# A streaming-encoder block on one core: seven head pairs' attention probabilities turned by VectorE in squares of 32, convolution taps moved around them, and a second residual buffer

## The reference

```python
h = rms_norm(x)                                   # one projection of h gives c_q, c_kv, k_rope, u, gates
q = rms_norm(c_q) @ w_uq;  k, v = split(rms_norm(c_kv) @ w_ukv)      # per head; rope on 64 columns
s = (q k^T) * scale                               # for each block of 128 queries
p = softmax(where(chunk(key) <= chunk(query), s, -inf))              # chunks of 64 tokens
y_a = p v
u = silu(layer_norm(causal_depthwise_conv(a * sigmoid(g), 31 taps)))
x = x + (sigmoid(gA) * y_a + sigmoid(gB) * (u @ w_pw2 + b)) @ w_o
x = x + cross_attention(rms_norm(x), rms_norm(mem))
x = x + swiglu(rms_norm(x))
```

## Time and profile before

| | |
|---|---|
| median of 3 runs | 1668.11 us |
| lowest, highest | 1668.08, 1668.18 us |
| the profiled execution | 1668.08 us |
| its span, first to last instruction | 1666.3 us |
| busy: TensorE, VectorE, ScalarE, GpSimd | 1651.1, 1128.5, 822.7, 104.7 us |

### The profile page before, as it was taken

One profiled execution on the slowest core, in us unless ns is written; L12 is line 12 of the kernel. 1 busy time (PEld: TensorE's weight loads), 2 busy tenths in 40 slices (PEclk: granted clock), 3 DMA queues, 4 the chain that ended last, 5 costly groups with the idle time before them and its releaser, 6 DMA issues.

```text
span 1666.3 us, 23809 instructions
## 1 busy us (share of the span) xinstructions
PE 1651.1 (99%) x7760; PEld 1378.8 (83%) x7760; DVE 1128.5 (68%) x1461; ACT 822.7 (49%) x1049; POOL 104.7 (6%) x154
## 2 busy tenths in 40 slices
PE   9999999999999999999999999999999999999997
PEld 8888888888888888878888888888888888888886
DVE  5578777778986467986558856666666666654453
ACT  7556555556545444556555644444444444344343
POOL 3100100010000000120001200000000000000000
PEclk9999999999999999999999999999999999999999
DMA  7865555556676665554435666666666666565563
GB/s 231 246 206 161 173 166 155 169 158 176 176 214 184 192 213 177 187 191 155 147 127 196 188 196 191 193 195 190 191 185 191 201 197 194 194 217 182 184 213 133
DMA packets 161106, 309.68 MB, mean 186 GB/s; under 512 B 10240, under 2 KB 16896, under 8 KB 160800
## 3 DMA queue, kind: packets, MB, share of 16 engines
q1 hardware_dynamic: 158864, 301.50, 59.0%
q0 software_dynamic: 1488, 6.42, 1.0%
q10 hardware_dynamic: 704, 1.11, 0.2%
HBM read 306.89 MB, written 2.10 MB: 185 GB/s over the span
## 4 chain that ended last, share of the span: by engine, by line
PE 92%; DVE 4%; issue 2%; ACT 1%; DMA 0%; DVEq 0%; POOL 0%; ACTq 0%; POOLq 0%; SPq 0%
PE acc L365 28%; PE acc L367 27%; PE acc L366 27%; DVE w_lo L1261 2%; PE tp L377 1%; DVE x_f L1600 1%; PE acc L582 1%; PE acc L580 1%; PE acc L581 1%; PE sc L492 1%; ACT w_hi L786 0%; PE ov L516 0%; PE sc L497 0%; DMA raw<-in_w_in_dram 0%; PE sc L506 0%
## 5 line engine op out<-in xcount | busy, mean ns | idle before, releaser
L1261 DVE TENSOR_TENSOR w_lo<-raw,w_hi 128x1024 fp32r<-128x1024 f32 (+3 forms) x591 | 718.7, 1221 | 428.9 <-ACT w_hi L786 419.5
L786 ACT ACTIVATE w_hi<-raw 128x1024 fp32r<-128x1024 f32 (+3 forms) x591 | 605.8, 1027 | 758.3 <-PE acc L367 722.3
L365 PE MATMUL acc<-w_hi,crossT 128*128 128x512 f32 x832 | 324.8, 390 | 0.8 <-DVEq L1618 0.7
L367 PE MATMUL acc<-w_hi,crossT 128*128 128x512 f32 x832 | 323.9, 389 | 0.0
L366 PE MATMUL acc<-w_lo,crossT 128*128 128x512 f32 x832 | 323.8, 389 | 0.0
L365 PE MATMUL acc<-w_hi,mixT 128*128 128x512 f32 x732 | 289.4, 395 | 1.6 <-ACTq L881 0.7
L367 PE MATMUL acc<-w_hi,mixT 128*128 128x512 f32 x732 | 285.5, 390 | 0.0
L366 PE MATMUL acc<-w_lo,mixT 128*128 128x512 f32 x732 | 285.1, 389 | 0.0
L365 PEld LDWEIGHTS acc<-w_hi,crossT 128*128 128x128 f32 x832 | 156.2, 188 | 33.9 <-issue 1.5
L367 PEld LDWEIGHTS acc<-w_hi,crossT 128*128 128x128 f32 x832 | 156.2, 188 | 32.6
L366 PEld LDWEIGHTS acc<-w_lo,crossT 128*128 128x128 f32 x832 | 156.2, 188 | 32.1
(11 more groups left out here) (267 smaller groups left out, 1552.8 us busy)
## 6 DMA issues: line engine op xcount, KB each, us to landing
raw<-in_w_in_dram SPq DMA_DIRECT2D x104, 512.0 KB, 4.3
raw<-in_w_gate_dram SPq DMA_DIRECT2D x88, 512.0 KB, 4.3
raw<-in_w_up_dram SPq DMA_DIRECT2D x88, 512.0 KB, 3.8
raw<-in_w_down_dram SPq DMA_DIRECT2D x80, 512.0 KB, 4.1
raw<-in_w_kv_mem_dram SPq DMA_DIRECT2D x64, 512.0 KB, 4.0
raw<-in_w_o_dram SPq DMA_DIRECT2D x32, 512.0 KB, 4.1
raw<-in_w_q_mem_dram SPq DMA_DIRECT2D x32, 512.0 KB, 3.7
raw<-in_w_o_mem_dram SPq DMA_DIRECT2D x32, 512.0 KB, 3.7
```

What stands on the lines that cost most here:

```text
L365: mm(o, lo, whi, start=first and k == 0, stop=False)
L367: ins = mm(o, hi, whi, start=False, stop=end)
L786: fn(w_hi[:, s, 0:width], raw[:, s, 0:width], ACT.Copy).then_inc(hi_done, 1)
L1261: V.tensor_tensor(w_lo[:, s, 0:width], raw[:, s, 0:width], w_hi[:, s, 0:width].bitcast(F32), ALU.subtract).then_inc(lo_done, 1)
```

## The change

- TensorE's six turns and ScalarE's copy for pairs 0 to 6 go. VectorE instead turns `probs` into `probsT` in 16 instructions of 32 partitions x 192 elements (six squares of 32 each): 5 behind its low part of tile 9, 5 behind tile 10's, 6 behind tile 11's. The last one raises `probs_out`.
- TensorE's value products move from behind tile 7 to behind tile 8, VectorE's gating from tile 7 to tile 9.
- The 20 taps per pass stay 20; in passes 1 to 6 they now stand 3, 3, 2, 2, 2, 0, 0, 0, 3, 0, 3, 2 behind tiles 0 to 11 (before 0, 2, 1, 1, 2, 2, 2, 2, 2, 2, 2, 2).
- The scores of the next pair wait for `scores_read` instead of `probs_out`.
- Pair 7 keeps the old way (`LAST_PE`, `LAST_ACT`, `LAST_DVE`). One of the memory operand's parts moves from pass 7 (behind tile 9) into the memory stage.
- `x_f` gets a second buffer, laid in `row_bc`, and the turn waits for the low part of two chunks before; the `x_update` loops are written out on ScalarE, VectorE and GpSimd.
- In `pointwise` VectorE adds the bias to the first half before the low part of a tile, the second half behind it.

```diff
-PAIR_PE = {1: (0, 1), 3: (2,), 6: (5,), 7: (7,)}
-PAIR_ACT = {1: (0, 1), 4: (3,), 6: (5,)}
-PAIR_DVE = {3: (2,), 4: (3,), 7: (7,)}
+PAIR_PE = {1: (0, 1), 3: (2,)}
+PAIR_ACT = {1: (0, 1), 4: (3,)}
+PAIR_DVE = {3: (2,), 4: (3,), 5: (4,), 6: (5,), 7: (6,), 9: (7,)}
...
                     tile_products(i * 12 + T_C, 8 + t, t, 2, cqT, 2 * t, 2, UQ, i * 3 + (C_C + 1))
+                    if t == 0 and not first:
+                        attention(7, i - 1, i + (Q_C - 1))
...
+                if t in (4, 5, 6):
+                    if t == 4:
+                        dve.wait_ge(exp_done, 4 * p + 4)
+                        if not (isinstance(p, int) and p == 0):
+                            dve.wait_ge(pv_done, p)
+                    for n in range((0, 5, 10)[t - 4], (5, 10, 16)[t - 4]):
+                        i, j = n // 4, n % 4
+                        src = probs[32 * i:32 * i + 32, :, :].rearrange("p h (j c) -> p (h j) c", c=P)
+                        to = probsT[32 * j:32 * j + 32, :, :].rearrange("p h (j c) -> p (h j) c", c=P)
+                        ins = V.transpose(to[:, :, 32 * i:32 * i + 32], src[:, :, 32 * j:32 * j + 32])
+                    if t == 6:
+                        ins.then_inc(probs_out, 1)
...
-            share = [0, 0, 2, 3, 4, 6, 8, 10, 12, 14, 16, 18, EARLY_TAPS]
+            share = [0, 3, 6, 8, 10, 12, 12, 12, 12, 15, 15, 18, EARLY_TAPS]
...
-                    if last and t in (9, 11):
-                        operand_lo(t // 2 - 2)
+                    if last and t == 11:
+                        operand_lo(2)
...
                 for t in range(4):
-                    split_lo(c * 4 + T_D, t + 4)
...
-                        for b in range(NB):
-                            bias_added(b, c, c + C_D, c * 4 + (T_D + 4), free)
+                        bias_added(0, c, c + C_D, c * 4 + (T_D + 4), free)
+                    split_lo(c * 4 + T_D, t + 4)
+                    if t == 2:
+                        bias_added(1, c, c + C_D, c * 4 + (T_D + 4), free)
...
                     dve.wait_ge(stage_full, fills)
-                    dve.wait_ge(x_lo_out, done)
+                    if done >= 2:
+                        dve.wait_ge(x_lo_out, done - 1)
...
-            with dve.Fori(1, 4) as c:
+            for c in range(1, 4):
```

More of the change, by code:

```diff
@@ L50 @@
 EARLY_TAPS = 20
-PAIR_PE = {1: (0, 1), 3: (2,), 6: (5,), 7: (7,)}
-PAIR_ACT = {1: (0, 1), 4: (3,), 6: (5,)}
-PAIR_DVE = {3: (2,), 4: (3,), 7: (7,)}
+PAIR_PE = {1: (0, 1), 3: (2,)}
+PAIR_ACT = {1: (0, 1), 4: (3,)}
+PAIR_DVE = {3: (2,), 4: (3,), 5: (4,), 6: (5,), 7: (6,), 9: (7,)}
+LAST_PE = {1: (0, 1), 3: (2,), 6: (5,), 7: (7,)}
+LAST_ACT = {1: (0, 1), 4: (3,), 6: (5,)}
+LAST_DVE = {3: (2,), 4: (3,), 7: (7,)}
 HEAD_PE = {0: (0,), 2: (1,), 5: (3,), 6: (4,)}
@@ L183, in program @@
         conv_age.close()
-        x_f = sb(middle, "x_f", [P, 4, TOK])
+        x_f = [sb(middle, "x_f", [P, 4, TOK])[:, :, :], row_bc[:, 0:4 * TOK].rearrange("p (k t) -> p k t", t=TOK)]
         memqT = [sb(middle, f"memqT{j}", [P, 4, TOK], F32R) for j in range(2)]
@@ L486, in attention @@
                     if not (isinstance(p, int) and p == 0):
-                        pe.wait_ge(probs_out, p)
+                        pe.wait_ge(scores_read, p)
                     blocks = ((0, P, 0), (P, TOK, P))
@@ L596, in _ @@
                 products(T_E, t, 8, *mem_rows(t), 2, CH, C_E)
-                for step in PAIR_PE.get(t, ()):
+                for step in LAST_PE.get(t, ()):
                     attention(step, PAIRS - 1, Q_LAST)
@@ L945, in attention @@
                 if t == 5:
-                    act.wait_ge(probs_turned, p + 1)
-                    if not (isinstance(p, int) and p == 0):
-                        act.wait_ge(pv_done, p)
+                    act.wait_ge(probs_turned, 1)
+                    act.wait_ge(pv_done, p)
                     fn(probsT[:, :, :], sc[:, :, 0:HALF], ACT.Copy).then_inc(probs_out, 1)
@@ L993, in gate_and_pair @@
                         operand_hi(t)
-                    if last and t == 9:
+                    if last and t == 11:
                         act.wait_ge(tile_done, i * 12 + (T_C + 8))
-                    if last and t in (9, 11):
-                        operand_hi(t // 2 - 2)
+                        operand_hi(2)
                     for step in PAIR_ACT.get(t, ()) if not first else ():
@@ L1035, in _ @@
                 split_hi(T_E, t + 4)
-                if t < 4:
-                    operand_hi(t + 4)
-                for step in PAIR_ACT.get(t, ()):
+                if t < 5:
+                    operand_hi(t + 3)
+                for step in LAST_ACT.get(t, ()):
                     attention(step, PAIRS - 1, Q_LAST)
@@ L1104, in x_part_hi @@
                 for k in range(4):
-                    ins = fn(x_f[:, k, :], x_f[:, k, :], ACT.Copy, scale=vcol(gain, c * 4 + k))
+                    ins = fn(x_f[done % 2][:, k, :], x_f[done % 2][:, k, :], ACT.Copy, scale=vcol(gain, c * 4 + k))
                 ins.then_inc(x_gained, 1)
                 act.wait_ge(x_gained, done + 1)
-                fn(crossT[0][:, cols(c * 4, 4), :], x_f[:, :, :], ACT.Copy).then_inc(x_hi_out, 1)
+                fn(crossT[0][:, cols(c * 4, 4), :], x_f[done % 2], ACT.Copy).then_inc(x_hi_out, 1)
             def x_update(c, tile0, done, s0, z0, norm, gain):
@@ L1123, in _ @@
                     x_squares(0, 2 * S_F, Z_F, R_CROSS)
-            with act.Fori(1, 4) as c:
+            for c in range(1, 4):
                 x_update(c, T_F, 0, S_F, Z_F, R_CROSS, "norm_cross")
@@ L1399, in attention @@
                     if not (isinstance(p, int) and p == 0):
-                        dve.wait_ge(probs_turned, p)
+                        dve.wait_ge(probs_out, p)
                     for h in range(2):
@@ L1424, in attention @@
                     ins.then_inc(branch_a, 1)
-            share = [0, 0, 2, 3, 4, 6, 8, 10, 12, 14, 16, 18, EARLY_TAPS]
+            share = [0, 3, 6, 8, 10, 12, 12, 12, 12, 15, 15, 18, EARLY_TAPS]
             share_first = [0, 0, 0, 0, 0, 6, 8, 10, 12, 14, 16, 18, EARLY_TAPS]
-            share_last = [0, 3, 6, 7, 9, 12, 15, 18, 18, 18, 19, 19, EARLY_TAPS]
+            share_last = [0, 3, 6, 8, 10, 13, 13, 13, 13, 16, 16, 19, EARLY_TAPS]
             def operand_lo(g):
@@ L1498, in _ @@
                 split_lo(T_E, t + 4)
-                if t < 4:
-                    operand_lo(t + 4)
-                for step in PAIR_DVE.get(t, ()):
+                if t < 5:
+                    operand_lo(t + 3)
+                for step in LAST_DVE.get(t, ()):
                     attention(step, PAIRS - 1, Q_LAST)
@@ L1598, in x_turn @@
                     src = stage[32 * i:32 * i + 32, :, :].rearrange("p b (k c) -> p b k c", c=P)
-                    dst = x_f[32 * j:32 * j + 32, :, :].rearrange("p k (b t) -> p b k t", b=NB)
+                    dst = x_f[done % 2][32 * j:32 * j + 32, :, :].rearrange("p k (b t) -> p b k t", b=NB)
                     ins = V.transpose(dst[:, :, :, 32 * i:32 * i + 32], src[:, :, :, 32 * j:32 * j + 32])
@@ L1929, in x_part_lo @@
                 hi, lo = (crossT[j][:, cols(c * 4, 4), :] for j in range(2))
-                G.tensor_tensor(lo, x_f[:, :, :], hi.bitcast(F32), ALU.subtract).then_inc(x_lo_out, 1)
+                G.tensor_tensor(lo, x_f[done % 2], hi.bitcast(F32), ALU.subtract).then_inc(x_lo_out, 1)
             for first_fill, norm, done in ((S_F, R_CROSS, 0), (S_H, R_FFN, 3)):
                 keep_x(0, 2 * first_fill + 2)
-                with gp.Fori(1, 4) as c:
+                for c in range(1, 4):
                     x_part_lo(c - 1, c + (done - 1))
```

## The result

| | before | after |
|---|---|---|
| median | 1668.09 us | 1693.57 us |
| lowest, highest | 1667.93, 1668.18 us | 1692.17, 1694.82 us |
| span of the profiled execution | 1666.3 us | 1692.7 us |
| TensorE busy | 1651.1 us | 1660.4 us |
| VectorE busy | 1128.5 us | 1165.7 us |

The changed kernel takes 1.0151 times as long as the one before, 95% interval 1.0139 to 1.0163: 25.5 us more. The forecast was 14 us more, with 1692 as the upper end of the range. The direction and the wait were right. The size was missed, and so was the range.

A forecast was written before the change was run, and what follows sets the result against it. TensorE, busy 1651.1 of 1666.3 us, was taken as the bound. Turns, new wait, key copy, first pointwise chunk and residual chunks summed as 1668.1 - 4.6 + 20.4 - 0.4 - 0.4 - 1.0 = 1682.1 us; range 1673 to 1692.

The forecast's parts named there:

- What leaves TensorE: Attention passes: the six turns cost TensorE 0.66 us per pair, so dropping them for seven pairs gives -4.6 us.
- The wait at the value products: Behind tile 8, TensorE waits for VectorE's last transposes: 2.4 us in pass 1, 3.0 in the others, +20.4 us.
- The price of a transpose: VectorE's 32x192 transposes in the attention passes: 0.38 us each, between 0.33 and 0.445.
- VectorE on time?: VectorE's list up to tile 11's low part: 27.9 us of work in 27.3 us, so 0.6 us late, not adding up.
- The rival: Clock falls in the new wait; value products and second query tile cost 3.3 us more, seven times: 1705 us; chance 5%.
- signs that the prediction named: Whole profile: value products waiting seven times, about 20 us; passes 36.3 us apart; transposes about 0.37 us; TensorE busy some 5 us less.
- The rest: Outside the turns and the new wait: -0.4 at the key copy, -0.4 at the first pointwise chunk, -1.0 at the residual chunks.
- The residual chunks: Four TensorE waits, 1.7 us together, shrink if written-out loops shorten GpSimd's copy: -1.0 us, between 0 and -1.7.
- The bias order: Pointwise stage: bias add ahead of a low part frees the accumulator sooner, -0.4 us at the first chunk, 0 elsewhere.
- The memory stage: The memory operand's part returns here, where VectorE is filled: 0 us, up to +1.0 if a low part comes late.
- The second buffer: Residual chunks: a second x_f gains nothing, since the wait it removes wasn't last.
- the saved turns to win: Rival in the attention passes: probabilities are ready when TensorE arrives, leaving 1661.6 us; chance 4%.

The follow-up runs named there:

- the kernel with ten transposes: The changed kernel without its last six transposes per pass, so part of the probabilities is left out; 1661.60 us, ratio 0.9961.
- the kernel with both moves: The changed kernel with the last six transposes ahead of tile 11's low part and the value products behind tile 9; 1662.18 us, ratio 0.9965.
- the old attention: The changed kernel with the attention passes as before the change, all else as changed; 1665.96 us, ratio 0.9987.
- the first experiment: The changed kernel with ten idle 128x128 products on TensorE, after tile 8 and ahead of the wait for the transposed probabilities; 1682.12 us, ratio 1.0081.

## Why the prediction missed

**What leaves TensorE**: 4.6 us forecast, 0.61 x 7 = 4.3 by the passes of the kernel with ten transposes. Right within 0.3.

**The wait at the value products**: right in place, cause and size. Forecast 2.4, five times 3.0, and 3.0; measured from start to start 2.4, 2.9 five times, 2.6; 20.4 against 19.5 us.

**The price of a transpose**: 0.38 us forecast from start to start, and 2.30 us for six is 0.38.

**VectorE on time?** Forecast 0.6 us late, measured 0.5, and a fresh start in every pass, as the 4.1 to 5.5 us of idle time show. The count of its load that I used in the experiments was slightly high (33.8 us per pass; the kernel with both moves runs passes of 33.56 with VectorE as the bound).

**The clock: the step that failed.** The rival was named, at the right place, but given 5% and left outside the range, because "TensorE has no idle time of 3 us in this trace ... so no row bounds it". That was a reason for more weight and not for less: a wait of a size that the trace of before doesn't contain is an unknown cost, and its upper bound belonged in the range. So the sum has no term for the products behind the wait. The fall occurred in every pass, and 3 us of idle time were not needed for it: 2.4 us were enough in pass 1, and 2.2 in four passes of the kernel with the last transposes sooner. As the rival put it (3.3 us per pass: all value products and the whole of tile 9 at half speed), the price was too high: the clock was back by the middle of tile 9 in five passes, late in it in pass 5 and only at its end in pass 4. It came to 1.4 to 1.6 us, 2.9 in pass 4, 12.3 us in all. The rival's 1705 is as far above the result as the forecast's 1682.1 is below.

With the clock held up, the forecast's sum is met: 1682.12 us measured. That it is met to a tenth is luck, since smaller errors cancel: the waits came 0.9 us below the forecast, the turns gave back 0.3 less, and the slower start of the value products at full clock, 0.7 us, stood nowhere. Two of the signs that the prediction named failed by the clock as well: passes 36.3 us apart (measured 37.5 to 38.0, and 39.2) and TensorE busy some 5 us less (9.3 more).

The rule of the Trainium skill that the prediction cites ("TensorE: Matmul & The Clock Gate", section "Why this matters for your kernels"), that idle gaps bring the lower level back, agrees with the trace: 0.54 behind a wait of 2.9 us.

**The rest**: -1.8 us forecast; -1.7 in the changed kernel (1.1 outside the passes, 0.6 off the key copy's wait) and -2.2 with the old attention. The total is right by luck, for the parts are not. The residual chunks gave 2.3 us (1.2 and 1.1 over the two sets), beyond the -1.7 that I allowed at most and not through GpSimd's copy. The bias order lost 0.2 on balance where I had -0.4. The memory stage took 0.6 more in its first chunk, inside the 0 to 1.0 that I allowed. The second buffer did nothing, as forecast.

**Slips in the working**, none of which moves the forecast: for the saved turns to win, 0.05 us is what all six transposes together might take, not each, as the bracket there has it. 1668.1 - 4.6 with the -1.8 of the rest is 1661.7. The waits at the ends add up to 15.3 and 27.4 us, where 15.5 and 28 were used.

## What to carry to other kernels

Before moving work from the engine that is the bound to one with room, follow the chain at the new place: what must be done last there, when can it start, and when does the bound engine arrive. Here 6 small transposes at the wrong place make the passes 27 us longer; with them one low part sooner and the value products one tile later, the same 16 transposes gain some 4 us (6 with the rest of the change). A new wait of TensorE that is longer than those in the trace of before has to be priced twice, once for itself and once for the products behind it at the lower clock: here 2.4 to 2.9 us, and mostly 1.6 on top. Where such a wait can't be avoided, idle products in it can pay, as the 11.5 us of the first experiment show.

## What the runs showed of the hardware

- The granted clock fell to 1.2 GHz behind every one of the seven idle stretches of 2.4 to 2.9 us in the changed kernel. With the last transposes sooner it fell behind four of five of 2.2 us, and not behind the fifth, nor behind those of 1.9 and 1.6 us. With the value products behind tile 9, where the idle stretches are 0.8 us or less, it never fell. So two idle stretches of one length can differ; the cost is then 1.6 us in one pass and 0 in another. The wider spread of the changed kernel, 2.7 us between its lowest and highest run against 0.3 before, fits this, but no run tests it.
- Behind the fall, products of 128x384 take 0.32 us from start to start and not 0.17, and the value products up to 2.58 us. At full clock they take 1.36 us behind a wait and 1.25 without one.
- A transpose of 32x192 takes 0.369 us in the median and one of 32x256 takes 0.436. A line through these two sizes, an estimate, gives about 1 ns per element and some 0.17 us besides.
- Work of the same shape can be dearer in a hardware loop: the distance from one dependent tap to the next is 0.66 us in the loop and 0.50 where it is written out, in the last pass of the kernel before and in all passes once VectorE's are written out. Why was not tested.
